# Two squared-ReLU MLPs on one TensorEngine: sums of h behind the next bank, the last set's work spread over seven down units, operands' highs ahead of the weights' highs

## The chip, the cores and the metric

The kernel runs on one core of one Trainium2 chip. The metric is the device time of one execution in microseconds (us). TensorE is PE below, VectorE DVE, ScalarE ACT, GpSimd POOL, SyncE SP.

## The reference

Two layers of a streaming encoder, each a mixer and an MLP, for 1024 prompt frames and 64 sample frames that share the weights. The change touches the MLPs alone:

```
def squared_relu_mlp(h, w_up, w_down):
    return jnp.square(jax.nn.relu(h @ w_up)) @ w_down

h = rms_norm(x, norm_g[i, 2])
x = x + rms_norm(squared_relu_mlp(h, mlp_w_up[i], mlp_w_down[i]), norm_g[i, 3])
```

With D_MODEL 1024 and D_FF 4096 an MLP turns 1088 frames of 1024 values into 4096 and back. All is fp32. The kernel makes each fp32 product out of three passes over two fp32r parts of each operand, a high (the operand rounded by a cast) and a low (the operand less its high): high by high, high by low, low by high.

## The kernel before

Frames are in columns, 1088 of them: T, in halves of 544 or in blocks of 384, 384 and 320. Class Mlp writes one MLP, and its methods tensor, scalar, vector, gpsimd and sync write what each engine does, in a fixed order. Engines wait for each other through counting semaphores; nothing is scheduled but by this code. The program has two MLPs (near 570 to 1290 us and 1700 to 2410 us).

**First wave and plain tiles.** The 32 tiles of 128 hidden values come in three kinds. FIRST_TILES, four of them, are made block by block in four banks while the norm of the next block still runs; DVE takes each bank (relu, L1620), ACT squares it (L1411). During the last block (b == NB - 1) ACT also writes three scaled copies of h for each pair k of its tiles (gain, L1389), and DVE makes from them the four sums of h that Strassen's scheme (in Winograd's form, seven products in place of eight) needs (sums_of_h, L1502 to L1509). Then come two PLAIN_TILES (dense_set, L314), on banks 0 to 2 and 5 to 7. PE begins the first of them when three of the last four first banks are taken and the lows of its weights are ready: cast by ACT (ws.high, L224), subtracted on POOL (ws.low, L230). Behind the plain tiles DVE makes the lows of the sums (L1513) and takes the plain banks (L1542), and the first double set begins (product, L1205).

**Double sets.** The other 26 tiles are 13 double sets (DOUBLES) of seven products each (N_PROD, product i in one of four slots of two banks). DVE combines them to the four blocks of the result (combine, L1552), takes relu (L1556, L1574), ACT squares (L1393), and DVE makes three sums and a difference of them (sums_of_act, L1530 to L1535). SP stores all to memory (store_set).

**Down.** The second matrix is worked in 7 groups (GROUPS) of 4 units (PAIRS), numbered d = 4g + p. A unit is again seven products of 12 matmuls, 1.5 us each at full clock, some 10.5 us a unit. Each product is added to y by DVE (take_product, L1600 for the first, L1604), which frees its slot for a later product: the take of product 0 is waited for by product 3 of the same unit, 1 by 4, 2 by 6, 3 and 4 by 0 and 1 of the next unit, 5 by its 5, 6 by its 2.

Each group needs seven operands (pieces), which SP loads one group ahead (load_piece), ACT casts to highs (high_piece, L1397), and DVE turns to lows (low_piece, L1513). Each unit needs one unit of weights, which SP loads when product 4 of the unit two before is done (load_pair, L210); POOL mixes it for Strassen's scheme (mix, L240 to L245), ACT casts it in two parts, the blocks as loaded (L251) and the mixed ones (L253), and POOL makes the lows (low_pair, L261). The last group loads the four first tiles in place of pieces (load_first, high_first, low_first), and its units end with turn_back, two subtractions on y (L1612).

What matters for the order: the last set's relus and sums are done in one go, the relus at the end of the last double set, the four sums behind the whole of down unit 0. In a down unit ACT casts the weights first and the pieces behind them. DVE subtracts the pieces at the places of this table, which counts as (p, i), behind the take of product i:

```
{(1, 2): 0, (1, 5): 1, (2, 1): 2, (2, 3): 3, (2, 5): 4, (3, 2): 5, (3, 5): 6}
```

Of the kernel before, what the change touches and what calls it, by code (L numbers as in the profile page):

```python
# [10 lines left out]
ALU = mybir.AluOpType  # L11
# [129 lines left out]
class WeightStream:  # L141
# [105 lines left out]
    def high_pair(self, act, unit):  # L247
# [3 lines left out]
        self.chip.nc.scalar.copy(hi[:, 0, QUARTER:UNIT], raw[:, 0, QUARTER:UNIT]).then_inc(self.pair_hi, 1)  # L251
        act.wait_ge(self.mixed, 3 * self.pair(unit) + 3)
        self.chip.nc.scalar.copy(hi[:, 1], raw[:, 1]).then_inc(self.pair_hi, 1)  # L253

# [770 lines left out]
class Mlp:  # L1025
# [25 lines left out]
    STEPS = 13  # L1051
# [37 lines left out]
    def step(self, n, k):  # L1089

        return self.steps(self.DOUBLE_STEP) + self.STEPS * n + k

# [207 lines left out]
    def sync(self, sp):  # L1300
# [61 lines left out]
        for g in range(GROUPS):  # L1362
            for p in range(PAIRS):
                d = PAIRS * g + p
                if g < GROUPS - 1 and p < 2:
                    for i in ((0, 1, 2), (3, 4, 5, 6))[p]:
                        load_piece(g + 1, i)
                elif p < 2:
                    for j in (2 * p, 2 * p + 1):
                        load_first(j)  # L1370
                sp.wait_ge(self.prod_full, self.down_count(d, 4))
                if d < PAIRS * GROUPS - 2:
                    ws.load_pair(sp, self.down_unit(d + 2))
                    if d == 0:
                        store_set(DOUBLES)
                    continue
# [5 lines left out]
    def scalar(self, act):  # L1382
# [49 lines left out]
        for n in range(DOUBLES):  # L1432
# [6 lines left out]
            last = n == DOUBLES - 1  # L1439
            ws.high_pair(act, self.down_unit(0) if last else self.double_unit(n + 1, 0))  # L1440
            if last:
                high_piece(0, 0)
            act.wait_ge(self.stepped, self.step(n, self.C11_TAKEN))
            square(self.act[:, 0])
            if last:
                high_piece(0, 1)
                high_piece(0, 2)
            else:
                ws.high_pair(act, self.double_unit(n + 1, 1))
            act.wait_ge(self.stepped, self.step(n, self.C12_TAKEN))  # L1450
            square(self.act[:, 2])
            if last:
                high_piece(0, 3)
            act.wait_ge(self.stepped, self.step(n, self.C22_TAKEN))
            square(self.act[:, 3])
            if last:
                high_piece(0, 4)
            act.wait_ge(self.stepped, self.step(n, self.C21_TAKEN))
            square(self.act[:, 1])
        high_piece(0, 5)  # L1460
        high_piece(0, 6)

        for g in range(GROUPS):
            for p in range(PAIRS):
                d = PAIRS * g + p
                if d < PAIRS * GROUPS - 1:
                    ws.high_pair(act, self.down_unit(d + 1))
                if g < GROUPS - 1:
                    for i in ((), (0, 1, 2), (3, 4), (5, 6))[p]:
                        high_piece(g + 1, i)  # L1470
                else:
                    for j in ((), (0, 1), (2, 3), ())[p]:
                        high_first(j)
# [19 lines left out]
    def vector(self, dve):  # L1493
# [30 lines left out]
        def sums_of_act(n, squares):  # L1524
# [3 lines left out]
            dve.wait_ge(self.squared, squares)  # L1528
            dve.wait_ge(self.a_out, self.outs(n))
            nc.vector.tensor_tensor(s1, a21, a22, ALU.add).then_inc(self.stepped, 1)  # L1530
            nc.vector.tensor_tensor(a21, a21, a11, ALU.subtract).then_inc(self.stepped, 1)
            dve.wait_ge(self.stepped, self.step(n - 1, self.SUM1))
            nc.vector.tensor_tensor(s2, s1, a11, ALU.subtract).then_inc(self.stepped, 1)
            dve.wait_ge(self.stepped, self.step(n - 1, self.SUM2))
            nc.vector.tensor_tensor(s4, s2, a12, ALU.subtract).then_inc(self.stepped, 1)  # L1535
# [23 lines left out]
        def double_until_c21(n):  # L1559

            c22, banks, last = self.halves(self.c22[:]), self.slot_banks, n == DOUBLES - 1
# [22 lines left out]
            relu(n, a12, a12, 0, self.C12_RAW)  # L1584
            relu(n, a22, self.c22[:], 1, self.C22_FULL)
            if last:
                low_piece(0, 3)
            full(n, 6)
            combine(n, self.C21_RAW, a21, c22, banks(6), ALU.subtract)
            relu(n, a21, a21, 1, self.C21_RAW)  # L1590
# [24 lines left out]
        for b in range(NB):  # L1615
            self.before.keep_ready(dve, b)
            for j in range(FIRST_TILES):
# [6 lines left out]
                if b == NB - 1:  # L1624
                    sums_of_h(j)
# [10 lines left out]
        sums_of_act(0, self.squares(PLAIN_TILES))  # L1636
        for n in range(DOUBLES):
            double_until_c21(n)
            if n < DOUBLES - 1:
                sums_of_act(n + 1, self.double_squares(n, 4))  # L1640

        for d in range(PAIRS * GROUPS):
            g, p = divmod(d, PAIRS)
            for i in range(self.N_PROD):
                take_product(d, i)
                if d == 0 and i < 3:
                    low_piece(0, 4 + i)
                if g < GROUPS - 1:
                    piece = {(1, 2): 0, (1, 5): 1, (2, 1): 2, (2, 3): 3, (2, 5): 4, (3, 2): 5, (3, 5): 6}.get((p, i))
                    if piece is not None:  # L1650
                        low_piece(g + 1, piece)
# [1699 lines left out]
```

## Time and profile before

| | us |
|---|---|
| median of 3 runs | 2456.99 |
| lowest and highest | 2453.17, 2457.27 |
| time of the profiled execution | 2461.53 |
| its span | 2459.7 |
| PE busy, share of the span | 2356.7, 96% |
| DVE busy | 1599.3, 65% |
| ACT busy | 1015.4, 41% |
| POOL busy | 966.1, 39% |
| mean granted clock of PE | 0.984 |

The span runs from the first to the last instruction of the profiled execution; 1.8 us lie around it. Busy is the time in which at least one instruction of the engine ran. The granted clock is the share of its 2.4 GHz that PE was given.

### The profile page before, as it was taken

To read this page: it belongs to the slowest core of one execution; us is meant where nothing else is said; L and a number is where in the kernel's file an instruction comes from. 1 tells how busy PE (TensorE), PEld (TensorE's weight loads), DVE (VectorE), ACT (ScalarE), POOL (GpSimd) and SP (SyncE) were. 2 spreads that over 40 slices of the span, in tenths; PEclk is the share of its full clock that TensorE was granted. 3 is DMA by queue.
4 is the path that set the end of the run, shared out by engine and by line. 5 is a ranking of instruction groups with operands and counts; after the bars stand their busy time and mean duration, and the time that the engine had idled before them with its cause. 6 is when DMAs were issued, how large, how long until landed. Compare 5 with 4: busy or idle time off the path is not lost.

```text
span 2459.7 us, 46195 instructions
## 1 busy us (share of the span) xinstructions
PE 2356.7 (96%) x18814; PEld 2215.0 (90%) x18814; DVE 1599.3 (65%) x2469; ACT 1015.4 (41%) x1910; POOL 966.1 (39%) x580
## 2 busy tenths in 40 slices
PE   8999999999899998999999999999999999999997
PEld 7888887799899998999999877689999999999997
DVE  6554454417777778778768344426687778787886
ACT  5554544536433334333326455536533334333321
POOL 0101020115344445677746200114244445677663
PEclk9999999999999999999999999899999999999999
DMA  3101011015243336343325100014323435434334
GB/s 114 44 10 59 19 42 35 30 48 162 94 147 146 146 138 225 134 151 107 133 74 162 60 21 27 26 35 130 123 107 147 146 147 192 163 123 162 115 109 133
DMA packets 117695, 257.42 MB, mean 105 GB/s; under 512 B 11264, under 2 KB 42240, under 8 KB 117536
## 3 DMA queue, kind: packets, MB, share of 16 engines
q1 hardware_dynamic: 109664, 248.62, 29.3%
q10 hardware_dynamic: 7808, 6.56, 0.9%
q8 instruction: 102, 1.67, 0.3%
q14 instruction: 57, 0.47, 0.1%
q0 software_dynamic: 64, 0.10, 0.0%
HBM read 176.79 MB, written 78.45 MB: 104 GB/s over the span
## 4 chain that ended last, share of the span: by engine, by line
PE 68%; DVE 12%; issue 7%; ACT 5%; DMA 4%; POOL 3%; ACTq 0%; SPq 0%; DVEq 0%; POOLq 0%
PE banks L1205 28%; PE banks L298 25%; PE banks L2446 4%; DMA w_raw<-in_units 4%; DVE y L1604 3%; POOL w_raw L240 1%; DVE mlp_s_lo L1513 1%; PE banks L2581 1%; ACT w_hi L253 1%; PE banks L2600 1%; PE banks L1956 1%; PE banks L1937 1%; PE banks L1924 1%; POOL w_raw L243 1%; ACT mlp_s_raw L1389 1%
## 5 line engine op out<-in xcount | busy, mean ns | idle before, releaser
L298 PE MATMUL banks<-h_hi,w_hi 128*128 128x384 f32 (+1 forms) x1416 | 487.8, 344 | 3.7 <-DVE w_lo L269 1.4
L298 PE MATMUL banks<-h_lo,w_hi 128*128 128x384 f32 (+1 forms) x1416 | 467.8, 330 | 0.0
L298 PE MATMUL banks<-h_hi,w_lo 128*128 128x384 f32 (+1 forms) x1416 | 467.2, 330 | 0.0
L230 POOL TENSOR_TENSOR w_lo<-w_raw,w_hi 128x1024 fp32r<-128x1024 f32 x56 | 139.1, 2483 | 800.7 <-ACT w_hi L224 800.7
L261 POOL TENSOR_TENSOR w_lo<-w_raw,w_hi 128x768 fp32r<-128x768 f32 (+1 forms) x164 | 372.4, 2293 | 184.5 <-DVE w_raw L245 147.2
L1604 DVE TENSOR_TENSOR y<-banks,y 128x544 f32<-128x544 f32 x360 | 259.9, 722 | 96.1 <-PE banks L1205 79.5
L1205 PE MATMUL banks<-h_hi,w_hi 128*128 128x272 f32 x1312 | 275.0, 291 | 28.1 <-DVE y L1604 10.2
L298 PEld LDWEIGHTS banks<-h_hi,w_hi 128*128 128x128 f32 x1416 | 268.1, 189 | 27.0 <-issue 18.6
L1205 PE MATMUL banks<-h_lo,w_hi 128*128 128x272 f32 x1312 | 272.2, 289 | 0.0
L1205 PE MATMUL banks<-h_hi,w_lo 128*128 128x272 f32 x1312 | 272.0, 289 | 0.0
L298 PEld LDWEIGHTS banks<-h_lo,w_hi 128*128 128x128 f32 x1416 | 268.3, 189 | 1.9
L298 PEld LDWEIGHTS banks<-h_hi,w_lo 128*128 128x128 f32 x1416 | 267.7, 189 | 0.0
L1205 PEld LDWEIGHTS banks<-h_hi,w_hi 128*128 128x128 f32 x1312 | 205.7, 189 | 33.0 <-DVE y L1600 10.1
L1205 PE MATMUL banks<-mlp_s_hi,w_hi 128*128 128x272 f32 x984 | 207.8, 293 | 16.8 <-DVE y L1604 13.5
L1205 PEld LDWEIGHTS banks<-h_lo,w_hi 128*128 128x128 f32 x1312 | 207.3, 190 | 0.0
L1205 PEld LDWEIGHTS banks<-h_hi,w_lo 128*128 128x128 f32 x1312 | 206.4, 190 | 0.0
L1205 PE MATMUL banks<-mlp_s_hi,w_lo 128*128 128x272 f32 x984 | 204.1, 290 | 0.0
L1205 PE MATMUL banks<-mlp_s_lo,w_hi 128*128 128x272 f32 x984 | 203.1, 288 | 0.0
L253 ACT CAST w_hi<-w_raw 128x1024 fp32r<-128x1024 f32 x82 | 86.3, 1053 | 266.2 <-POOL w_raw L245 157.8
L261 POOL TENSOR_TENSOR wide_lo<-wide_raw,wide_hi 128x768 fp32r<-128x768 f32 (+1 forms) x52 | 118.1, 2292 | 146.3 <-DVE wide_raw L245 146.3
L1205 PEld LDWEIGHTS banks<-mlp_s_hi,w_hi 128*128 128x128 f32 x984 | 154.4, 190 | 23.2 <-DVE y L1604 16.3
L251 ACT CAST w_hi<-w_raw 128x768 fp32r<-128x768 f32 x82 | 68.4, 834 | 245.4 <-DMA w_raw<-in_units 245.4
(252 smaller groups left out, 5054.4 us busy)
## 6 DMA issues: line engine op xcount, KB each, us to landing
w_raw<-in_units SPq DMA_DIRECT2D x154, 512.0 KB, 3.7
sets_scratch<-mlp_act SPq DMA_DIRECT2D x28, 1088.0 KB, 4.2
h_raw<-sets_scratch SPq DMA_DIRECT2D x56, 544.0 KB, 5.3
sets_scratch<-mlp_act_sums SPq DMA_DIRECT2D x28, 816.0 KB, 5.0
mlp_s_raw<-sets_scratch SPq DMA_DIRECT2D x42, 544.0 KB, 6.4
wide_raw<-in_units SPq DMA_DIRECT2D x26, 512.0 KB, 4.4
x_scratch<-y SPq DMA_DIRECT2D x48, 192.0 KB, 2.4
norm_x<-x_scratch SPq DMA_DIRECT2D x28, 192.0 KB, 3.2
```

Of the source, the lines that this page charges most:

```text
L230: c.nc.gpsimd.tensor_tensor(c.w_lo[:, s], c.w_raw[:, s], c.w_hi[:, s].bitcast(F32), ALU.subtract).then_inc(self.ready, 1)
L240: ops.tensor_tensor(two(to[:, 0:2 * QUARTER]), of(raw, 0)[:, None, :].to_broadcast([P, 2, QUARTER]), two(raw[:, QUARTER:3 * QUARTER]), ALU ...
L243: ops.tensor_tensor(of(to, 2), of(raw, 2), of(to, 0), ALU.subtract).then_inc(self.mixed, 1)
L251: self.chip.nc.scalar.copy(hi[:, 0, QUARTER:UNIT], raw[:, 0, QUARTER:UNIT]).then_inc(self.pair_hi, 1)
L253: self.chip.nc.scalar.copy(hi[:, 1], raw[:, 1]).then_inc(self.pair_hi, 1)
L261: self.chip.nc.gpsimd.tensor_tensor(lo[:, i, at], raw[:, i, at], hi[:, i, at].bitcast(F32), ALU.subtract).then_inc(self.pair_ready, 1)
L298: mm = chip.nc.tensor.matmul(out, w, x, start=(first and n == 0), stop=(last and n == 2))
L1205: mm = nc.tensor.matmul(chip.banks[:, bank + c, 0:half], w, x[:, c * half:(c + 1) * half], start=(not prod.adds and n_k == 0 and m == 0), ...
L1389: nc.scalar.activation(self.operand(i, k, None, self.s_raw), chip.y[:, 2 * k + tile, self.HALVES[half]], ACT.Copy, scale=gains[tile]).then ...
L1513: nc.vector.tensor_tensor(out, raw, high.bitcast(F32), ALU.subtract).then_inc(self.a_ready, 1)
L1604: nc.vector.tensor_tensor(y, bank, y, ALU.add).then_inc(self.y_added, 1)
L2446: mm = nc.tensor.matmul(out, x, y, start=(k == 0 and i == 0), stop=(k == KT - 1 and i == 2))
```

## The change

Nothing is computed in another way, and no instruction's shape changes. Five things move, in both MLPs:

1. First wave, last block: sums_of_h(j) stands behind the take of bank j + 1 rather than of bank j; on ACT gain(j) stands ahead of the wait for bank j's take, and the casts of the two plain units come behind banks 2 and 3 rather than 1 and 2.
2. The last set (n == DOUBLES - 1): its three late relus go from the end of the set to down units 0, 1 and 2 (behind product 6 of unit 0, else behind product 3), its four sums from behind unit 0 to units 3, 4, 5 and 6. ACT's last four squares go to units 0 to 3. step() is renumbered to fit, and SP stores the last set at unit 8 in place of unit 0.
3. ACT in down units: the pieces' highs stand ahead of the weights' highs. In the last set the blocks of down unit 1 are cast ahead of pieces 5 and 6 (high_blocks), its mixed part behind them (high_mixed).
4. DVE in down units: the lows of pieces stand behind products 1 and 5 of units p = 1, 2, 3, and the seventh behind product 1 of the next group's first unit, so no unit has more than two.
5. SP loads pieces 0 to 3 in a group's first unit and 4 to 6 in its second, rather than 0 to 2 and 3 to 6.

```diff
@@ step
+        if isinstance(n, int) and n == DOUBLES - 1:
+            k = {self.C21_RAW: self.C12_TAKEN, self.C12_TAKEN: self.C22_TAKEN, self.C22_TAKEN: self.C21_RAW}.get(k, k)
@@ sync
-                    for i in ((0, 1, 2), (3, 4, 5, 6))[p]:
+                    for i in ((0, 1, 2, 3), (4, 5, 6))[p]:
                         load_piece(g + 1, i)
...
-                    if d == 0:
+                    if d == 2 * PAIRS:
                         store_set(DOUBLES)
@@ scalar
                 n = FIRST_TILES * b + j
+                if b == NB - 1:
+                    gain(j)
                 act.wait_ge(self.first_taken, self.firsts(n + 1))
...
-                if b == NB - 1:
-                    gain(j)
-                    if j in (1, 2):
-                        ws.high(act, u0 + FIRST_TILES + j - 1)
+                if b == NB - 1 and j > 1:
+                    ws.high(act, u0 + FIRST_TILES + j - 2)
...
+        ws.high_pair(act, self.down_unit(0))
+        for i in range(5):
+            high_piece(0, i)
+        ws.high_blocks(act, self.down_unit(1))
+        for i in range(5, self.N_PROD):
+            high_piece(0, i)
...
+                if p == 0 and g:
+                    high_piece(g, 6)
+                if p and g < GROUPS - 1:
+                    for i in (2 * p - 2, 2 * p - 1):
+                        high_piece(g + 1, i)
+                elif p in (1, 2):
+                    for j in (2 * p - 2, 2 * p - 1):
+                        high_first(j)
+                if 0 < d < PAIRS * GROUPS - 1:
                     ws.high_pair(act, self.down_unit(d + 1))
...
+                elif d == 0:
+                    ws.high_mixed(act, self.down_unit(1))
+                if g == 0:
+                    i, taken = last_squares[p]
+                    act.wait_ge(self.stepped, self.step(DOUBLES - 1, taken))
+                    square(self.act[:, i])
@@ vector
-                if b == NB - 1:
-                    sums_of_h(j)
+                if b == NB - 1 and j:
+                    sums_of_h(j - 1)
+        sums_of_h(FIRST_TILES - 1)
...
+                if d < self.LAST_STEPS and i == (6 if d == 0 else 3):
+                    last_set(d)
                 if d == 0 and i < 3:
                     low_piece(0, 4 + i)
+                if g and p == 0 and i == 1:
+                    low_piece(g, 6)
                 if g < GROUPS - 1:
...
+                    if p and i in (1, 5):
+                        low_piece(g + 1, 2 * (p - 1) + (i == 5))
...
-            if d == 0:
-                sums_of_act(DOUBLES, self.double_squares(DOUBLES - 1, 4))
```

PE and POOL have the same instructions in the same order as before. DVE, last block of the first wave of the first MLP, before: each bank's take (mlp_first_act<-banks) is followed by the four sums of h.

```order
L1620 SCALAR_TENSOR_TENSOR mlp_first_act<-banks,keep 128x320
L1502 SCALAR_TENSOR_TENSOR mlp_s_raw<-y,gains,mlp_s_raw 128x544
L1504 SCALAR_TENSOR_TENSOR mlp_s_raw<-y,gains,mlp_s_raw 128x544
L1507 TENSOR_TENSOR mlp_s_raw<-mlp_s_raw 128x544
L1509 TENSOR_TENSOR mlp_s_raw<-mlp_s_raw 128x544
L1620 SCALAR_TENSOR_TENSOR mlp_first_act<-banks,keep 128x320
```

The same place of DVE now:

```order
L1654 SCALAR_TENSOR_TENSOR mlp_first_act<-banks,keep 128x320 x2
L1513 SCALAR_TENSOR_TENSOR mlp_s_raw<-y,gains,mlp_s_raw 128x544
L1515 SCALAR_TENSOR_TENSOR mlp_s_raw<-y,gains,mlp_s_raw 128x544
L1518 TENSOR_TENSOR mlp_s_raw<-mlp_s_raw 128x544
L1520 TENSOR_TENSOR mlp_s_raw<-mlp_s_raw 128x544
L1654 SCALAR_TENSOR_TENSOR mlp_first_act<-banks,keep 128x320
```

The third bank's take has one block of sums ahead of it, where it had two. DVE, end of down unit 0 and start of unit 1, before (y<-banks is a take, mlp_act_sums and mlp_act<-mlp_act the last set's sums):

```order
L1600 COPY y<-banks 128x544 x2
L1604 TENSOR_TENSOR y<-banks,y 128x544
L1600 COPY y<-banks 128x544
L1530 TENSOR_TENSOR mlp_act_sums<-mlp_act 128x544
L1531 TENSOR_TENSOR mlp_act<-mlp_act 128x544
L1533 TENSOR_TENSOR mlp_act_sums<-mlp_act_sums,mlp_act 128x544
L1535 TENSOR_TENSOR mlp_act_sums<-mlp_act_sums,mlp_act 128x544
L1600 COPY y<-banks 128x544
L1604 TENSOR_TENSOR y<-banks,y 128x544 x2
L1513 TENSOR_TENSOR h_lo<-h_raw,h_hi 128x2x544
```

And now:

```order
L1634 COPY y<-banks 128x544 x2
L1638 TENSOR_TENSOR y<-banks,y 128x544
L1634 COPY y<-banks 128x544
L1575 SCALAR_TENSOR_TENSOR mlp_act<-mlp_act,keep 128x544
L1634 COPY y<-banks 128x544
L1638 TENSOR_TENSOR y<-banks,y 128x544
L1524 TENSOR_TENSOR h_lo<-h_raw,h_hi 128x2x544
L1638 TENSOR_TENSOR y<-banks,y 128x544
L1634 COPY y<-banks 128x544
L1575 SCALAR_TENSOR_TENSOR mlp_act<-mlp_c_103,keep 128x544
L1634 COPY y<-banks 128x544
```

One relu stands where four sums stood, and the next unit has one relu more. ACT, down units 1 and 2, before (w_hi a cast of weights, h_hi and mlp_s_hi casts of pieces):

```order
L251 CAST w_hi<-w_raw 128x768
L253 CAST w_hi<-w_raw 128x1024
L1397 CAST h_hi<-h_raw 128x2x544 x2
L1397 CAST mlp_s_hi<-mlp_s_raw 128x2x544
L251 CAST w_hi<-w_raw 128x768
L253 CAST w_hi<-w_raw 128x1024
```

And now, in the units of a later group:

```order
L1407 CAST h_hi<-h_raw 128x2x544 x2
L251 CAST w_hi<-w_raw 128x768
L256 CAST w_hi<-w_raw 128x1024
L1407 CAST mlp_s_hi<-mlp_s_raw 128x2x544
L1407 CAST h_hi<-h_raw 128x2x544
L251 CAST w_hi<-w_raw 128x768
```

The pieces' casts, which stood behind the mixed weights' cast, stand ahead of both casts of the unit.

## Rows read from the trace of the kernel before

**Rows 1.** The page's part 1: busy us (share of the span) and instructions of each engine.

```profile
PE 2356.7 (96%) x18814; PEld 2215.0 (90%) x18814; DVE 1599.3 (65%) x2469; ACT 1015.4 (41%) x1910; POOL 966.1 (39%) x580
```

**Rows 2.** Waits of PE: who waited for whom, us in total, times, longest us.

```profile
PE banks L1205 <- DVE y L1604: 23.7, 32, 1.6
PE banks L1205 <- DVE y L1600: 11.7, 6, 3.0
PE banks L314 <- DVE mlp_first_act L1620: 8.6, 2, 4.3
PE banks L1205 <- DVE mlp_act L1542: 6.5, 2, 4.4
...
PE banks L1205 <- DVE h_lo L1513: 1.8, 2, 0.9
```

**Rows 3.** Windows: us; busy of PE, PEld, DVE, ACT, POOL; granted clock; DMA.

```profile
639.00:649.00 10.00, 9.98 (x46) 10.00 (x47) 5.39 (x5) 5.41 (x9) 2.74 (x1) 0.75 0.55 195
667.50:677.50 10.00, 9.95 (x67) 9.95 (x68) 7.07 (x10) 5.63 (x8) 2.75 (x2) 0.83 0.16 55
986.90:996.90 10.00, 9.91 (x60) 9.91 (x61) 6.28 (x9) 3.04 (x3) 4.18 (x2) 0.73 0.19 46
1766.70:1776.70 10.00, 9.97 (x51) 10.00 (x52) 5.43 (x5) 5.37 (x9) 2.77 (x1) 0.83 0.56 197
1796.90:1806.90 10.00, 9.97 (x67) 9.97 (x68) 7.10 (x11) 5.64 (x8) 0.93 (x1) 0.83 0.28 91
2092.10:2102.10 10.00, 10.00 (x58) 10.00 (x59) 6.58 (x8) 0.56 (x1) 1.54 (x1) 0.70 0.97 356
```

**Rows 4.** Timeline of DVE, first wave: start, us, line, operation [idle before <- releaser].

```profile
634.97 2.74 DVE L1507 TENSOR_TENSOR mlp_s_raw<-mlp_s_raw 128x544 f32<-128x544 f32 x1
...
638.39 0.48 DVE L1620 SCALAR_TENSOR_TENSOR mlp_first_act<-banks,keep 128x320 f32<-128x320 f32 x1
```

**Rows 5.** Timeline of PE, the first matmuls of the first plain tile.

```profile
639.02 1.24 PE L314 MATMUL banks<-h_hi,w_hi 128*128 128x384 f32 x3 [4.31 <-DVE mlp_first_act L1620]
```

**Rows 6.** Timeline of ACT, last block of the first wave.

```profile
625.54 2.02 ACT L1389 ACTIVATE mlp_s_raw<-y,gains 128x544 f32<-128x544 f32 x3
...
633.33 1.03 ACT L224 CAST w_hi<-w_raw 128x1024 fp32r<-128x1024 f32 x1
```

**Rows 7.** Timeline of POOL, lows of the first plain unit.

```profile
634.44 2.70 POOL L230 TENSOR_TENSOR w_lo<-w_raw,w_hi 128x1024 fp32r<-128x1024 f32 x1 [16.25 <-ACT w_hi L224]
```

**Rows 8.** Timeline of DVE behind the first wave: lows of the sums, first plain take.

```profile
655.21 11.03 DVE L1513 TENSOR_TENSOR mlp_s_lo<-mlp_s_raw,mlp_s_hi 128x1632 fp32r<-128x1632 f32 x4
666.16 1.34 DVE L1542 SCALAR_TENSOR_TENSOR mlp_act<-banks,keep 128x768 f32<-128x768 f32 x2
```

**Rows 9.** Timeline of DVE, the last set's sums in down unit 1.

```profile
955.98 1.44 DVE L1530 TENSOR_TENSOR mlp_act_sums<-mlp_act 128x544 f32<-128x544 f32 x1
...
961.95 0.71 DVE L1600 COPY y<-banks 128x544 f32<-128x544 f32 x1
```

**Rows 10.** Timeline of DVE, lows of pieces in down units 4 and 5.

```profile
996.27 1.28 DVE L1513 TENSOR_TENSOR h_lo<-h_raw,h_hi 128x1088 fp32r<-128x1088 f32 x1
...
1013.41 3.33 DVE L1513 TENSOR_TENSOR h_lo<-h_raw,h_hi 128x1088 fp32r<-128x1088 f32 x1 [0.61 <-ACT h_hi L1397]
...
1018.95 2.39 DVE L1513 TENSOR_TENSOR h_lo<-h_raw,h_hi 128x1088 fp32r<-128x1088 f32 x1
```

**Rows 11.** Timeline of POOL, the weights of down unit 6.

```profile
1008.36 1.30 POOL L240 TENSOR_TENSOR w_raw<-w_raw 128x512 f32<-128x512 f32 x1 [3.11 <-DMA w_raw<-in_units]
...
1011.37 4.23 POOL L261 TENSOR_TENSOR w_lo<-w_raw,w_hi 128x768 fp32r<-128x768 f32 x2
```

**Rows 12.** Timeline of PE, down unit 6, product 0.

```profile
1022.03 0.52 PE L1205 MATMUL banks<-mlp_s_hi,w_hi 128*128 128x272 f32 x2 [1.02 <-DVE y L1604]
```

**Rows 13.** Timeline of ACT, pieces' highs behind the weights' in down unit 5.

```profile
1012.28 2.10 ACT L1397 CAST h_hi<-h_raw 128x1088 fp32r<-128x1088 f32 x2
```

**Rows 14.** The page's part 6, pieces' loads: xcount, KB each, median us to landing.

```profile
h_raw<-sets_scratch SPq DMA_DIRECT2D x56, 544.0 KB, 5.3
```

More of the change, by code:

```diff
@@ L251, in high_pair, with high_mixed @@
         self.chip.nc.scalar.copy(hi[:, 0, QUARTER:UNIT], raw[:, 0, QUARTER:UNIT]).then_inc(self.pair_hi, 1)
+    def high_mixed(self, act, unit):
+        hi, _, raw = self.tiles(self.place(unit))
         act.wait_ge(self.mixed, 3 * self.pair(unit) + 3)
         self.chip.nc.scalar.copy(hi[:, 1], raw[:, 1]).then_inc(self.pair_hi, 1)
+    def high_pair(self, act, unit):
+        self.high_blocks(act, unit)
+        self.high_mixed(act, unit)
     def low_pair(self, pool, unit):
@@ L1438, in scalar @@
             nc.scalar.copy(self.halves(self.c22[:]), self.slot_banks(0)).then_inc(self.copied, 1)
[L1439 to L1442, printed above, removed]
+            if n == DOUBLES - 1:
+                break
+            ws.high_pair(act, self.double_unit(n + 1, 0))
             act.wait_ge(self.stepped, self.step(n, self.C11_TAKEN))
             square(self.act[:, 0])
[L1445 to L1461, printed above, removed]
+            ws.high_pair(act, self.double_unit(n + 1, 1))
+            for i, taken in ((2, self.C12_TAKEN), (3, self.C22_TAKEN), (1, self.C21_TAKEN)):
+                act.wait_ge(self.stepped, self.step(n, taken))
+                square(self.act[:, i])
[5 more added lines that the diff above has]
+            high_piece(0, i)
+        last_squares = ((0, self.C11_TAKEN), (2, self.C12_TAKEN), (3, self.C22_TAKEN), (1, self.C21_TAKEN))
         for g in range(GROUPS):
@@ L1583, in double_until_c21, with last_set @@
             combine(n, self.C12_RAW, a12, c22, banks(4), ALU.subtract, self.C22_FULL)
-            relu(n, a12, a12, 0, self.C12_RAW)
-            relu(n, a22, self.c22[:], 1, self.C22_FULL)
             if last:
                 low_piece(0, 3)
+            else:
+                relu(n, a12, a12, 0, self.C12_RAW)
+                relu(n, a22, self.c22[:], 1, self.C22_FULL)
             full(n, 6)
             combine(n, self.C21_RAW, a21, c22, banks(6), ALU.subtract)
-            relu(n, a21, a21, 1, self.C21_RAW)
+            if not last:
+                relu(n, a21, a21, 1, self.C21_RAW)
+        def last_set(n):
+            a11, a21, a12, a22 = (self.act[:, i] for i in range(4))
+            if n == 0:
+                relu(DOUBLES - 1, a12, a12, 0, self.C12_RAW)
+            elif n == 1:
+                relu(DOUBLES - 1, a22, self.c22[:], 1, self.C22_FULL)
+            elif n == 2:
+                relu(DOUBLES - 1, a21, a21, 1, self.C21_RAW)
+            else:
+                sum_of_act(DOUBLES, n - 3)
         def take_product(d, i):
@@ L1635, in vector @@
         take_plain(1)
-        sums_of_act(0, self.squares(PLAIN_TILES))
+        sums_of_act(0)
         for n in range(DOUBLES):
@@ L1639, in vector @@
             if n < DOUBLES - 1:
-                sums_of_act(n + 1, self.double_squares(n, 4))
+                sums_of_act(n + 1)
         for d in range(PAIRS * GROUPS):
```

40 lines of the change are left out of this document (19 added, 21 removed).

## The prediction

> **What bounds the kernel now.** I read the page first, then PE's waits, the windows, and the timelines of the places that the waits name. PE is busy for 2356.7 of 2459.7 us [rows 1], so any gain has to come out of the 103 us in which PE stands, or out of time at a lower clock. The waits of PE say who keeps it [rows 2]. Five kinds lie in what the change touches: takes of down products (L1604, 23.7 us in 32 waits, and L1600, 11.7 in 6), lows of pieces (L1513, 1.8), the third first-tile bank (L1620, 8.6 in 2), and the first plain bank (L1542, 6.5 in 2). That is 52.3 us, all of it waits for DVE, though DVE is busy for only 65% of the span: it is late, not overfull. Behind the long stops PE's granted clock is below 1. Six windows of 10 us have 0.75, 0.83, 0.73, 0.83, 0.83 and 0.70 [rows 3], that is a part of each at 1.2 GHz and the rest at 2.4. PE is busy throughout them, so each costs 10 x (1 - clock): 2.5, 1.7, 2.7, 1.7, 1.7 and 3.0, together 13.3 us. So 65.6 us are there to be had.
>
> **First wave and plain tiles.** PE stands 4.31 us ahead of the first plain tile, until the take at 638.39 [rows 4, 5]. That take stood behind two blocks of sums, and each block waited for ACT's copies (2.02 us, [rows 6]), one of its operations also for POOL, whose first plain lows run from 634.44 to 637.14 (2.74 us for that operation, [rows 4, 7]). Now one block stands ahead of the third take, and its copies come before the takes. The third bank was full one product before 634.7 (24 matmuls of 320 columns, 3.2 us at 2.4 GHz), at about 631.3, so it is taken by 632. But then something else is last: the lows of the plain weights. ACT casts them behind the square of bank 2, at about 632.2 to 633.2 (before: 633.33, [rows 6]), and POOL needs 2.7 us [rows 7]. PE starts at about 636.1 and still stands 1.4 of the 4.3 us.
>
> The next stop is no longer set there. The double sets begin when DVE has taken the first plain bank, behind four lows (11.03 us, [rows 8]). The whole chain on DVE moves forward. Its lows began at 655.2 [rows 8], some 3 us of mixing behind the last sum. Now the four blocks of sums run at about 3.0 us each (four operations of 0.7 to 0.8) from 628.2, with two short takes and one or two waits for POOL of 2 us between them. That gives about 645, and the lows at 648: 7 us earlier, in both MLPs alike, and the double sets start 7.0 us earlier, at 660.5 in the first. PE itself gets there at 636.1 + 24.0 = 660.1: before, it ran from 639.0 until 2.1 us before the take's end at 667.5, which is 26.4 us [rows 2, 5, 8], less 2.5 of clock. Term: 2 x 7.0 = **14.0 us**, clock of the plain tiles included. Ends: 5 each if DVE's lows meet POOL worse (they took 1.5 us more in the second MLP), 7.4 if PE's own arrival decides. Behind it PE lost 1.7 us of clock twice [rows 3]. The stop shrinks from 2.0 to about 0.4 in the first MLP, and from 4.4 to some 2 in the second. I count one of the two: **1.7 us**.
>
> **Last set's relus and sums.** Before, four sums stand ahead of unit 1's first take and last from 955.98 to 961.95, 6.0 us with the waits for POOL [rows 9]. PE stands for the first take 3.0 us [rows 2]. The three late relus delay the lows of pieces 3 to 6 too (the 1.8 us of L1513). All seven are now single operations of 0.7 us, at most one to a unit. The take of product 3 is asked for by the next unit's first product 4.5 us later, so 0.7 us, or 0.7 + 2.4 behind the longer of POOL's two lows (4.23 together, [rows 11]), fits. What is moved on SP: store_set goes from unit 0 to unit 8. Its 1.9 MB stood ahead of the weights of unit 3, which came late. At unit 8 it stands ahead of unit 9's three pieces and the weights of unit 11, which may land some 2 us later; these have 3.6 us to spare (below). ACT's squares are waited for only by the sums, three units on. Cost nothing.
>
> **Steady down units.** In unit 5 the first low waits 0.61 us for ACT, because the piece's cast stands behind the weights' mixed cast [rows 10, 13], and then for POOL: 3.33 us for what took 1.28 at 996.27, since POOL works from 1011.37 to 1015.60 [rows 10, 11]. The next low at 1018.95 also takes 2.39, and product 2 of unit 6 stands 1.02 us [rows 12] for the take of product 6. Units with three lows do the same. Now the piece is cast a unit ahead, and no unit has three lows. By these rows, counted from a unit's start: take 1 ends at 3.75, where POOL is between its mix and its lows. If DVE wins, its low ends at 5.0, if POOL wins at 6.9; take 2 ends at 7.6 at the latest and is asked for at 9.0. The low behind take 5 falls from 9.7 to 11.0, when POOL is idle (it starts the next mix at 11.3). Take 6 ends at 11.7 and is asked for at 13.5. Hence no stop in a plain unit. In units 1 to 6 a relu or sum makes three again. The same reckoning leaves 0.3 us for take 6 when all three meet POOL. Before, such units stood some 1 us [rows 12]; I let 5 of 12 do so: 5 us remain. The last group's lows come earlier on ACT by the same move. Term: 23.7 + 11.7 + 1.8 - 5.0 = **32.2 us**, ends 18 (half stays) and 37. With the cluster of long stops in units 1 to 3 gone, its clock returns: 2.7 + 3.0 = **5.7 us**, ends 0 and 5.7.
>
> What the order costs the weights: on ACT two casts of pieces (2.10 us, [rows 13]) stand ahead of the weights' casts. They run before the weights land, since POOL waits 3.1 us for its load in each unit [rows 11]. If not: POOL's lows end at 1015.6 and product 1 of unit 6 needs them at 1019.2, so 3.6 us are free.
>
> **Sum**: 14.0 + 1.7 + 32.2 + 5.7 = 53.6 us. The profiled execution took 2461.5, 4.5 above the median of 2457.0; against the median, **2403.4 us**.
>
> **Rivals.** *The stops move to POOL's port.* Rows show that a DVE operation with two inputs in SBUF waits for POOL's running instruction [rows 10, 11], while one that reads banks does not. If meetings are worse than reckoned, each of the 14 moved operations costs 1 us, and the 36 units with two lows 0.3 each: 25 stay in place of 5, and 2423; with the clock's 5.7 gone too, 2429. The Trainium skill, "SBUF — State Buffer", section "Who interferes with whom", says that a DVE instruction with two SBUF inputs and a GpSimd one that reads SBUF exclude each other for a whole instruction. The trace agrees (3.33 us against 1.28). By that rule alone, 14 operations that each wait 2.4 us put up to 33 us back on DVE, and the result would be near 2437 if none of it were covered. For the forecast speaks that every take has 1.8 to 4.5 us before it is asked for.
>
> *The clock stays low.* The shorter stops might still be followed by 1.2 GHz. In the trace stops near 1 us in down units left it at 1, but a 2.0 us stop gave a window of 0.83 [rows 2, 3]. Without any clock 2411; inside the forecast.
>
> *Nothing gained*: another chain as late as DVE's, POOL's lows, stands just behind, and stops keep their length under another name. Against: 3.6 us free. 2457.
>
> *Slower*: ACT stops in order at a piece that has not landed, and the weights' casts, POOL's lows and PE queue behind it. A piece takes 5.3 us to land [rows 14] and is issued over 10 us before its turn. To decide, 36 units would have to lose over 1.5 us each beyond the 3.6 free, pieces some 5 us behind ACT's turn. At 6 us: 36 x 2.4 = 86 us more, 2490.
>
> **Chances.** Forecast (2390 to 2412) 0.64; port 0.23 (2412 to 2437); nothing gained 0.06, of which 0.04 within 0.2%; slower 0.05; lower than 2390 0.02. About 0.2% (5 us) is what a measurement of this kernel tells from no change. Faster 0.91, same 0.04, slower 0.05. Range 2390 to 2430: it takes in the forecast and most of the port's case.
>
> **What would show it.** PE's waits for L1620 (now L1654) near 3 us or put down to the plain weights' lows; waits for L1542 under 3; those for takes under 10 in all, with none above 1.5; windows behind the old stops at 0.95 and up; takes of product 6 less than 1.8 us behind their banks in steady units. Wrong: waits named after POOL's or ACT's w_lo and w_hi, DVE lows still at 3.3 us with stops behind them, or a long stop at units 10 and 11.

## The result, and the profile after

| | us |
|---|---|
| changed kernel, median of 4 runs | 2389.09 |
| lowest and highest | 2385.79, 2392.34 |
| kernel before, median of 4 runs | 2457.13 |
| ratio, 95% interval | 0.9721, 0.9695 to 0.9747 |
| its profiled execution, its span | 2392.34, 2390.6 |

The change takes off 68.0 us, where 53.6 were forecast. The sign and the mechanisms were right. The time is 0.9 us below the low end of the range, so the gain was mis-sized. The term that failed is the one of the down units' stops: each stop was priced at its idle row alone, and costs some 0.27 us more (below).

The page's part 1 and the first line of its part 4 (the chain of waits by engine), as in [rows 1]:

```profile
PE 2334.2 (98%) x18814; PEld 2203.1 (92%) x18814; DVE 1540.5 (64%) x2469; ACT 1015.4 (42%) x1910; POOL 980.7 (41%) x580
...
PE 87%; DVE 8%; issue 2%; ACT 2%; ACTq 0%; DMA 0%; POOL 0%; SPq 0%; DVEq 0%; POOLq 0%
```

PE's idle time fell from 103 us to 56. DVE does the same 2469 instructions and is busy 58.8 us less: it spends less time inside operations that wait for POOL. PE's waits, with the columns of [rows 2]:

```profile
PE banks L506 <- DVE norm_diag L737: 6.0, 6, 1.8
...
PE banks L321 <- POOL w_lo L230: 2.9, 2, 1.4
...
PE banks L1215 <- DVE y L1638: 2.2, 4, 0.9
...
PE banks L1215 <- DVE h_lo L1524: 0.4, 2, 0.2
```

The takes' 35.4 us of [rows 2] (23.7 and 11.7) are 2.2 us. The third first-tile bank is no longer waited for (8.6 us before), nor is the first plain bank (6.5). What stands in place of the former is the plain weights' lows, 1.4 us each, as predicted to the tenth. The largest wait left belongs to a norm, which the change does not touch.

Windows behind the places of [rows 3], same columns. The last is 60 us of down units:

```profile
637.70:647.70 10.00, 9.91 (x59) 9.91 (x60) 9.81 (x12) 3.56 (x4) 2.91 (x2) 1.00 0.55 164
665.30:675.30 10.00, 9.88 (x78) 9.85 (x79) 8.61 (x14) 2.35 (x3) 0.00 (x0) 1.00 0.36 136
940.00:1000.00 60.00, 60.00 (x483) 59.94 (x482) 50.86 (x57) 24.82 (x28) 50.05 (x28) 1.00 0.51 180
```

All are at the full 2.4 GHz, and the second MLP's are too. In those 60 us of down units PE does not stop once.

The first wave on DVE's timeline (start, us), against [rows 4, 8]:

```profile
632.87 0.49 DVE L1654 SCALAR_TENSOR_TENSOR mlp_first_act<-banks,keep 128x320 f32<-128x320 f32 x1
...
635.55 2.77 DVE L1520 TENSOR_TENSOR mlp_s_raw<-mlp_s_raw 128x544 f32<-128x544 f32 x1
...
649.57 11.04 DVE L1524 TENSOR_TENSOR mlp_s_lo<-mlp_s_raw,mlp_s_hi 128x1632 fp32r<-128x1632 f32 x4
660.54 1.34 DVE L1561 SCALAR_TENSOR_TENSOR mlp_act<-banks,keep 128x768 f32<-128x768 f32 x2
```

The third bank is taken at 632.87, not at 638.39. One sum still waits 2 us inside its operation for POOL. The four lows take the same 11.0 us as in [rows 8], but begin 5.6 us earlier, and the first plain bank is free (661.88) just before PE comes for it (661.94), without a stop.

And DVE's groups by shape, in 200 us of down units (xcount, busy us, mean ns, idle before):

```profile
L1524 DVE TENSOR_TENSOR h_lo<-h_raw,h_hi 128x1088 fp32r<-128x1088 f32 x19 | 30.8, 1621 | 0.0
L1524 DVE TENSOR_TENSOR mlp_s_lo<-mlp_s_raw,mlp_s_hi 128x1088 fp32r<-128x1088 f32 x15 | 22.1, 1474 | 0.0
```

Of the kernel before, the same in 1000 to 1210 us:

```profile
L1513 DVE TENSOR_TENSOR h_lo<-h_raw,h_hi 128x1088 fp32r<-128x1088 f32 x19 | 43.5, 2289 | 3.3 <-ACT h_hi L1397 3.3
L1513 DVE TENSOR_TENSOR mlp_s_lo<-mlp_s_raw,mlp_s_hi 128x1088 fp32r<-128x1088 f32 x14 | 33.2, 2375 | 4.0 <-ACT mlp_s_hi L1397 4.0
```

A low costs 1.5 to 1.6 us instead of 2.3 to 2.4, and none waits for ACT. This pair of views says most about the down units.

**Where the 69.1 us of span went.** I cut PE's timeline at three events: the end of the first wave's last matmul, the first matmul of the double sets, and the end of the last down matmul. S1 is the stretch between the first two, S2 between the last two. Every experiment below is read the same way. A stop is a row of PE's timeline with more than 0.1 us of idle before it, and that idle is what its row says.

| | S1, first and second MLP | S2 | stops in S2, their idle us |
|---|---|---|---|
| before | 32.84, 34.51 | 597.77, 596.41 | 23 and 23, 20.2 and 18.3 |
| after | 25.58, 25.58 | 569.20, 569.20 | 3 and 3, 1.3 and 1.3 |
| gain | 7.3 + 8.9 = 16.2 | 28.6 + 27.2 = 55.8 | |

The rest of the program took 2.9 us more, in stretches whose order is unchanged. In a later profile of the same kernel (below) the first wave ended 2.8 us earlier than in this one, so such a difference is within what they vary.

### The profile page after: what moved, and what is told of

Same layout as the page of the kernel before. It is cut to its first block, busy times and chain, and to the rows that moved or that the text cites. A ratio compares the mean times of both kernels' runs of the same rounds, so it can differ in the third digit from the quotient of the medians.

```text
span 2390.6 us, 46195 instructions
## 1 busy us (share of the span) xinstructions
PE 2334.2 (98%) x18814; PEld 2203.1 (92%) x18814; DVE 1540.5 (64%) x2469; ACT 1015.4 (42%) x1910; POOL 980.7 (41%) x580
## 4 chain that ended last, share of the span: by engine, by line
PE 87%; DVE 8%; issue 2%; ACT 2%; ACTq 0%; DMA 0%; POOL 0%; SPq 0%; DVEq 0%; POOLq 0%
PE banks L1215 45%; PE banks L305 26%; PE banks L2482 4%; DVE mlp_s_lo L1524 1%; PE banks L2617 1%; PE banks L2636 1%; PE banks L1992 1%; PE banks L1973 1%; DVE y L1638 1%; PE banks L1960 1%; PE banks L2000 1%; PE banks L2626 1%; DVE norm_acc L697 1%; DVE y L748 1%; PE banks L2601 1%
## 5 line engine op out<-in xcount | busy, mean ns | idle before, releaser
L268 POOL TENSOR_TENSOR w_lo<-w_raw,w_hi 128x768 fp32r<-128x768 f32 (+1 forms) x164 | 410.6, 2524 | 169.5 <-DVE w_raw L245 144.0
```

What stands on the lines that cost most here:

```text
L268: self.chip.nc.gpsimd.tensor_tensor(lo[:, i, at], raw[:, i, at], hi[:, i, at].bitcast(F32), ALU.subtract).then_inc(self.pair_ready, 1)
```

## The experiments

Two theories stood at the start. A: each part gives what its removed idle and its clock say, plus something that every stop costs and no wait row shows. B: the excess over the forecast came from one place, such as the clock or the wave. The mechanism, that DVE is late because it waits for ACT's order and for POOL's port, had to be shown as well.

### e1_wave: part 1 alone

```diff
 before.py, scalar
+                if b == NB - 1:
+                    gain(j)
                 act.wait_ge(self.first_taken, self.firsts(n + 1))
...
 vector
-                if b == NB - 1:
-                    sums_of_h(j)
+                if b == NB - 1 and j:
+                    sums_of_h(j - 1)
+        sums_of_h(FIRST_TILES - 1)
```

> The kernel before with the first part of the change alone (sums of h behind the next bank, gains ahead of the takes, plain weights cast behind banks 2 and 3). Theory A, that PE's stops cost what their idle rows say plus about 0.28 us each (the overlap of back-to-back matmuls and the restart) plus the clock behind them: the stretch from the first wave's end to the first double set goes from 32.8 and 34.5 us to 25.6 in both MLPs, and the stretch behind it, without its clock of 0.83, loses some 1.7 us each: in all 20 us less, near 2437. Theory B, that the parts only work together because DVE is late for another reason as well: less than half of it, 2447 or more.

Measured: 2438.96 against 2460.14, ratio 0.9926 (0.9903 to 0.9948), 21.2 us off. S1 is 25.59 in both MLPs, S2 593.10 and 594.87 with 23 and 21 stops. The wave is worth its 16 us by itself. The rest lies in S2, most of it clock: the window at the double sets' start is at 1.00 here, and three windows behind stops in S2 (0.84, 0.83, 0.83) give 5.0 us where the four of [rows 3] in S2 gave 9.1. Theory A had 20 us.

### e2_steady: parts 3 to 5 alone

```diff
 before.py, scalar
-                if d < PAIRS * GROUPS - 1:
-                    ws.high_pair(act, self.down_unit(d + 1))
-                if g < GROUPS - 1:
-                    for i in ((), (0, 1, 2), (3, 4), (5, 6))[p]:
+                if p == 0 and g:
+                    high_piece(g, 6)
+                if p and g < GROUPS - 1:
+                    for i in (2 * p - 2, 2 * p - 1):
                         high_piece(g + 1, i)
...
+                if d < PAIRS * GROUPS - 1:
+                    ws.high_pair(act, self.down_unit(d + 1))
 sync
-                    for i in ((0, 1, 2), (3, 4, 5, 6))[p]:
+                    for i in ((0, 1, 2, 3), (4, 5, 6))[p]:
 vector
+                if g and p == 0 and i == 1:
+                    low_piece(g, 6)
...
-                    piece = {(1, 2): 0, (1, 5): 1, (2, 1): 2, (2, 3): 3, (2, 5): 4, (3, 2): 5, (3, 5): 6}.get((p, i))
+                    if p and i in (1, 5):
+                        low_piece(g + 1, 2 * (p - 1) + (i == 5))
```

> The kernel before with parts 3 to 5 alone (pieces' highs ahead of the weights', two lows to a unit, pieces 0 to 3 and 4 to 6), the last set as before. Theory A: some 16 stops in each MLP from down unit 5 on go, 12 us of idle rows and 16 x 0.28 of uncounted time each, in all 31 to 33 us less, near 2425. Theory C, that idle rows are the whole price of a stop: 24 us less, near 2433. The 3.0 us stop behind the last set's sums stays, and with it perhaps the clock of 0.73 and 0.70 behind it.

Measured: 2417.59 against 2460.14, ratio 0.9834 (0.9809 to 0.9858), 42.6 us off, some 10 more than theory A had and 19 more than theory C. Of 23 stops an MLP, four and five are left. The long one is the wait behind the four sums, still there because part 2 is not:

```profile
958.20 0.41 PE L1205 MATMUL banks<-mlp_s_lo,w_hi 128*128 128x272 f32 x2
958.45 0.41 PE L1205 MATMUL banks<-mlp_s_hi,w_lo 128*128 128x272 f32 x2
961.88 0.52 PE L1205 MATMUL banks<-h_hi,w_hi 128*128 128x272 f32 x2 [3.02 <-DVE y L1602]
```

The window behind it:

```profile
961.90:971.90 10.00, 10.00 (x80) 10.00 (x81) 8.57 (x11) 0.75 (x1) 2.16 (x2) 1.00 0.85 305
```

In e1_wave a stop of the same length has:

```profile
954.70:964.70 10.00, 9.97 (x68) 9.97 (x69) 7.38 (x9) 0.59 (x1) 1.57 (x1) 0.84 0.99 358
```

So the stops at unit 3, which I had put down to the last set, went with the steady order alone, but for one of 0.22 us. The clock behind the 3.0 us stop happened to stay up.

### e3_lastset: part 2 alone

```diff
 after.py, vector (the wave, ACT's order in down units and SP's loads are put back in the same way)
-                if g and p == 0 and i == 1:
-                    low_piece(g, 6)
...
-                    if p and i in (1, 5):
-                        low_piece(g + 1, 2 * (p - 1) + (i == 5))
+                    piece = {(1, 2): 0, (1, 5): 1, (2, 1): 2, (2, 3): 3, (2, 5): 4, (3, 2): 5, (3, 5): 6}.get((p, i))
+                    if piece is not None:
+                        low_piece(g + 1, piece)
```

> The kernel before with part 2 alone (relus and sums of the last set spread over units 0 to 6, its ACT order, the store at unit 8), first wave and steady order of before. Theory A: the stops of units 0 to 4 (8.1 us of rows in the first MLP), their uncounted 0.28 each and the clock behind them (2.7 and 3.0 us) go, 22 us in all, near 2435. Rival: units that already have three lows get a fourth operation, and 12 units stand 1 us longer each: 10 us less only, near 2447.

Measured: 2449.22 against 2460.14, ratio 0.9958 (0.9943 to 0.9973), 10.9 us off. This is the rival's case. The 3.0 us stop is gone, but product 2 now waits 0.94, 1.02 and 1.10 us in units 2, 3 and 4, behind units in which DVE has two or three lows and one operation of the last set more. Alone, the spread pays part of its gain back. Beside the table with two lows to a unit and ACT's new order it does not: in the changed kernel no take makes PE wait in units 1 to 25. The three parts alone give 21.2 + 42.6 + 10.9 = 74.7; together they give 68.0 to 71.6, so they overlap little.

### e4_weights_first: the changed kernel with the weights' highs first

```diff
 after.py, scalar
+                if 0 < d < PAIRS * GROUPS - 1:
+                    ws.high_pair(act, self.down_unit(d + 1))
+                elif d == 0:
+                    ws.high_mixed(act, self.down_unit(1))
                 if p == 0 and g:
                     high_piece(g, 6)
...
-                if 0 < d < PAIRS * GROUPS - 1:
-                    ws.high_pair(act, self.down_unit(d + 1))
-                elif d == 0:
-                    ws.high_mixed(act, self.down_unit(1))
```

> The changed kernel with ACT casting the weights ahead of the pieces again, all else as changed. Theory A: the pieces' highs of a unit come behind the mixed weights' cast, some 4.8 us into the unit, so the low behind take 1 is late, misses POOL's pause between mix and lows, and take 2 comes about 1 us too late for product 6: 36 stops of 1 us and 0.28, near 2435. Rival, that the order on ACT is worth nothing as long as no unit has three lows: 2389.

Measured: 2461.36 in one run, so the whole gain is gone. Each MLP has 45 stops in S2 (23.4 and 25.5 us idle); S2 is 602.88 and 606.40. In 1000 to 1210 us, by shape:

```profile
L1524 DVE TENSOR_TENSOR h_lo<-h_raw,h_hi 128x1088 fp32r<-128x1088 f32 x19 | 48.9, 2572 | 12.1 <-ACT h_hi L1407 12.1
L1524 DVE TENSOR_TENSOR mlp_s_lo<-mlp_s_raw,mlp_s_hi 128x1088 fp32r<-128x1088 f32 x14 | 41.0, 2927 | 13.4 <-ACT mlp_s_hi L1407 13.4
```

ACT, POOL and DVE in one unit (this kernel's timeline, engine by engine):

```profile
1007.61 1.06 ACT L256 CAST w_hi<-w_raw 128x1024 fp32r<-128x1024 f32 x1 [3.19 <-POOL w_raw L245]
1008.57 1.09 ACT L1407 CAST mlp_s_hi<-mlp_s_raw 128x1088 fp32r<-128x1088 f32 x1
...
1007.65 4.22 POOL L268 TENSOR_TENSOR w_lo<-w_raw,w_hi 128x768 fp32r<-128x768 f32 x2
...
1009.70 3.33 DVE L1524 TENSOR_TENSOR mlp_s_lo<-mlp_s_raw,mlp_s_hi 128x1088 fp32r<-128x1088 f32 x1 [1.24 <-ACT mlp_s_hi L1407]
```

The mixed cast waits for POOL's mix. What stands behind it comes just when POOL starts its lows, and DVE's low then waits 1.2 us for ACT and 2 us inside its operation for POOL. I had expected 46 of these 72 us. With all else as changed, the order on ACT decides whether anything is gained.

### e5_old_table: the changed kernel with the old places of the lows

```diff
 after.py, scalar
-                    for i in (2 * p - 2, 2 * p - 1):
+                    for i in ((), (0, 1), (2, 3, 4), (5, 6))[p]:
-                if p == 0 and g:
-                    high_piece(g, 6)
...
 vector: the table of before, in place of the lows behind takes 1 and 5
```

> The changed kernel with the lows of pieces on DVE at their old places (three in units p = 2) and ACT casting them just ahead, before the weights. Theory A: units with three lows stand again, about 0.3 to 1 us in 12 to 24 of them, near 2400. Rival, that the places are worth nothing once ACT is on time: 2389.

Measured: 2404.72 in one run; 7 and 8 stops, S2 574.93 and 577.29. The lows take 1.9 us on average here, and none waits for ACT. So ACT's order carries most of the steady part and the places the rest, some 16 us by the totals and 13.8 by S2.

### e8_pool_writes: is it POOL's port?

The kernel before, with POOL's lows of the double and down weights replaced by a memset. This leaves out the low parts of those weights. POOL then has less to do too, and reads less.

```diff
 before.py, low_pair
-            self.chip.nc.gpsimd.tensor_tensor(lo[:, i, at], raw[:, i, at], hi[:, i, at].bitcast(F32),
-                                              ALU.subtract).then_inc(self.pair_ready, 1)
+            self.chip.nc.gpsimd.memset(lo[:, i, at].bitcast(F32), 0.0).then_inc(self.pair_ready, 1)
```

> The kernel before with POOL's lows of the double and down weights replaced by memsets to zero (low parts of these weights are left out of the products). POOL then reads SBUF only in its mixing. Port theory: the lows on DVE that took 3.3 and 2.4 us take 1.3 to 2, the stops from unit 5 on fall from some 16 an MLP to under 5, 25 us or more less, 2430 or below. Rival, that DVE is late because of ACT's order: lows still start late, stops stay, 2450 or more.

Measured: 2409.26 against 2459.09, one run each. S1 is 30.43 and 29.92, S2 576.19 and 574.74, with 6 and 4 stops. In 1000 to 1200 us:

```profile
L1512 DVE TENSOR_TENSOR h_lo<-h_raw,h_hi 128x1088 fp32r<-128x1088 f32 x20 | 25.7, 1284 | 3.4 <-ACT h_hi L1396 3.4
L1512 DVE TENSOR_TENSOR mlp_s_lo<-mlp_s_raw,mlp_s_hi 128x1088 fp32r<-128x1088 f32 x15 | 19.3, 1288 | 3.4 <-ACT mlp_s_hi L1396 3.4
```

Every low takes its bare 1.28 us, though DVE's and ACT's order is that of before. That is 50 us with nothing moved. One low there runs beside a memset, 1011.94 to 1013.22:

```profile
1011.94 1.28 DVE L1512 TENSOR_TENSOR mlp_s_lo<-mlp_s_raw,mlp_s_hi 128x1088 fp32r<-128x1088 f32 x1
```

```profile
1012.00 0.74 POOL L261 MEMSET w_lo<- 128x768 f32 x1
```

It is not held up. The 15 lows that overlap a memset in this trace take 1.28 to 1.33 us; the 53 that overlap only the subtractions of L261 in the trace of before take 1.28 to 3.35, 2.62 on average. The Trainium skill, "SBUF — State Buffer", section "Who interferes with whom", says that a DVE instruction with two SBUF inputs contends with a GpSimd one that reads SBUF and not with one that only writes; the trace agrees, at 1.28 us beside a memset and 3.33 beside a subtraction. Since POOL is also busy for less time here (624.1 us, not 966.1), it is these overlaps that separate port from load, not the total.

### e6_stops6 and e7_stops5: what a stop costs

The changed kernel, with six or five more additions on DVE that read product 0's bank, ahead of its take, in the first unit of groups 3, 4 and 5. Their results are used nowhere. They make three stops an MLP of a known length.

```diff
 after.py, take_product
+            if i == 0 and p == 0 and 3 <= d // PAIRS <= 5:
+                dve.wait_ge(self.a_out, self.outs(SETS))
+                for out in [self.act[:, n] for n in range(4)] + [self.act_sums[:, n] for n in range(6 - 4)]:
+                    nc.vector.tensor_tensor(self.halves(out), bank, self.halves(chip.keep[:, first]), ALU.add)
```

> The changed kernel with six more operations on DVE (each adds a bank and keep into space that is free by then, 0.65 us apart) ahead of the take of product 0 in the first unit of groups 3, 4 and 5 of both MLPs: work that the result does not need. PE then stands at product 3, some 1.6 us by its idle row. Theory A: the stretch from the first product of the double sets to the last of the down units grows from 569.2 by three times the idle row plus 0.28, to about 574.8. Theory C: by three times the idle row, to about 574.0.

> As the run with six, with five more operations: the stops are 0.65 us shorter, about 1.0 us by their rows. Theory A: the stretch is three times the row plus 0.28 above 569.2, about 573.0; the difference between row and cost is the same as with six. Theory C: about 572.2. If the uncounted part grew with the stop, it would be half as large here as with six.

Measured: 2401.76 and 2391.42, one run each, with stops of 1.69 and 1.06 us. From one made stop to the next, four units on, it is 43.85 and 43.21 us in the traces: 0.64 us more for 0.63 us more idle. So a longer stop costs just its longer row. Every stop costs something beside it, too. In both profiles of the changed kernel, without made stops, the same four units take 41.87 us: the stops cost 1.98 and 1.34 us, 0.29 and 0.28 more than their rows.

By the lengths that were expected the two theories could not be told apart: S2 is 574.72 and 573.64 with six operations (A 574.8, C 574.0), 571.82 and 571.73 with five (A 573.0, C 572.2). The 569.2 from which both counted holds a stop of 0.93 us at unit 27 that only the first of these four has. The totals say less still: 4.8 of the 10.3 us between them lie in S2, the rest where the edit does nothing. PE's timeline of e7_stops5:

```profile
1061.93 0.41 PE L1215 MATMUL banks<-mlp_s_lo,w_hi 128*128 128x272 f32 x2
1062.18 0.41 PE L1215 MATMUL banks<-mlp_s_hi,w_lo 128*128 128x272 f32 x2
1063.65 0.52 PE L1215 MATMUL banks<-h_hi,w_hi 128*128 128x272 f32 x2 [1.06 <-DVE y L1642]
1064.00 0.41 PE L1215 MATMUL banks<-h_lo,w_hi 128*128 128x272 f32 x2
```

A pair of matmuls lasts 0.41 us, but the next pair starts 0.25 behind it. The row's 1.06 us count from the end of the last pair (1062.18 + 0.41 = 1062.59), which lies 0.16 behind the time at which the next would have started. Behind the stop the first pair takes 0.35 us to the next one, 0.10 more than 0.25. Together 0.26. The ends of matmuls are modelled in these views, so how the 0.26 us divide is less sure than their sum, which rests on starts. From 1062.18 to 1064.00 it is 1.82 us where 0.50 would do: 1.32, not 1.06.

The lengths of S2 agree. The second MLP of the changed kernel's second run (below) is 567.94 with 0.35 us idle. Against it e7_stops5 has 571.73 with 3.39, so 0.75 us over three stops are not in the rows, 0.25 each; e6_stops6 has 573.64 with 5.29, 0.25 each. The 43 additional stops of each MLP of e4_weights_first give 0.28 and 0.27, once the 1.6 us of clock behind a stop of 3.51 us in its second MLP (window 0.84) are taken off. Over all 24 MLPs of the twelve traces, S2 less its idle and its clock is 567.1 us and 0.27 more for each stop, to within 0.6 us.

### after_again: the changed kernel once more

> The changed kernel once more, to stand beside the next run on the same chip: 2389, ratio 0.972.

Measured: 2386.92 (5 runs) against 2458.54 (9 runs), ratio 0.9714 (0.9701 to 0.9728). S1 is 25.59 and 25.60, S2 569.61 and 567.94. One stop of 1.6 us, for the weights of down unit 2, is new, and the 0.93 us at the end of the down units is gone. Such single stops come and go between runs; the lengths of the stretches do not change by more than 2 us.

### e9_better: can what is left be had?

```diff
 after.py, scalar
                 if b == NB - 1:
                     gain(j)
+                    if j > 1:
+                        ws.high(act, u0 + FIRST_TILES + j - 2)
...
 vector
             low(self.s_lo[:, r], self.s_raw[:, r], self.s_hi[:, r], self.operands(k + 1))
-        take_plain(0)
+            if k == 1:
+                take_plain(0)
...
+                if g == GROUPS - 1 and p and i == 3:
+                    turn_back(p - 1)
...
-            if g == GROUPS - 1:
+            if g == GROUPS - 1 and p == PAIRS - 1:
                 turn_back(p)
```

> The changed kernel with three more moves: the plain weights' casts ahead of ACT's wait for the take of banks 2 and 3, the first plain bank taken behind the second of the four lows, and turn_back of a unit behind take 3 of the next. Theory A: PE's wait for the plain lows falls from 1.43 to about 0.4, the double sets start that much earlier, and the stop of 0.93 (with its uncounted 0.28) goes: 2 x (1.0 + 1.4) = 4.8 us below the changed kernel, near 2384. Rival: DVE's chain of lows decides the start of the double sets anyway, and only turn_back's stop is gained: 2.6 us.

Measured: 2395.74 (5 runs), ratio 0.9739 (0.9724 to 0.9754), 9 us slower than the change. The plain tiles do start at once, and S1 falls to 24.13. But PE's waits now have a new first line of the MLP:

```profile
PE banks L1215 <- POOL wide_lo L268: 4.7, 2, 2.5
```

POOL has two pairs of lows to make ahead of the double sets:

```profile
654.38 7.20 POOL L268 TENSOR_TENSOR w_lo<-w_raw,w_hi 128x768 fp32r<-128x768 f32 x2 [14.91 <-ACT w_hi L251]
661.54 5.13 POOL L268 TENSOR_TENSOR wide_lo<-wide_raw,wide_hi 128x768 fp32r<-128x768 f32 x2
```

They come later themselves: 18.5 us behind the end of the first wave (654.38 against 635.89), where the changed kernel has 16.0 (652.38 against 636.36). Two of DVE's operations ahead of the last bank's take now wait for POOL (2.94 and 2.82 us), where one did:

```profile
633.51 2.94 DVE L1515 SCALAR_TENSOR_TENSOR mlp_s_raw<-y,gains,mlp_s_raw 128x544 f32<-128x544 f32 x1
...
637.24 2.82 DVE L1520 TENSOR_TENSOR mlp_s_raw<-mlp_s_raw 128x544 f32<-128x544 f32 x1
```

The take, ACT's square, the store behind it and the casts that wait for that store all follow. The double sets start 1.45 us earlier and meet lows that are 2.5 us late. Turning the result back inside the units gave stops of 0.8, 1.0 and 0.7 us, where the changed kernel has one of 0.9 in one profile and none in the other. Of the 10.8 us by which the spans differ, S1 and S2 hold 5.5; the rest lies where nothing was edited. This order does not give the 1.43 us of the plain tiles; whether another would was not tried. None of the kernels run beats the change.

## Why the prediction fell short, term by term

The profiled execution gained 69.1 us by its span. By the sum's own terms:

| term | predicted | measured |
|---|---|---|
| wave, S1 | 14.0 | 16.2 |
| idle of stops in S2 | 32.2 | 38.5 - 2.6 = 35.9 |
| clock in S2 | 1.7 + 5.7 | 9.1 |
| what a stop costs beside its row | 0 | 10.8 |
| other stretches | 0 | -2.9 |
| sum | 53.6 | 69.1 |

- **The step that failed is the down term, 23.7 + 11.7 + 1.8 - 5.0 = 32.2.** It took the idle in the rows of the waits for the whole price of a stop. For each MLP, what is left of S2's change once idle and clock are taken off is 5.3 and 5.5 us, over 20 stops that went: 0.27 us each. This is what the made stops show, 0.26 us in PE's timeline around one and 0.28 by four whole units. The same lines lay in the trace before: the duration of a pair there is 0.41 us as well, and the restart of [rows 12], which is product 2's, has 0.52.
- **The 5.0 us kept in units with three operations were not there.** The idle left is 2.2 us for takes, all of it in units 26 and 27, where turn_back stands, and none in units 1 to 6. The lows of the pieces average 1.5 to 1.6 us. Before, PE's idle in S2 also held 1.3 us of other kinds, which the sum had left out.
- **The wave's term was 2.2 us short.** The first MLP gave 7.3 for 7.0, the second 8.9. The forecast took both alike; the longer stop of 4.4 us, which the second MLP had at the start of its double sets, went entirely. PE's own arrival decided, the case for which 7.4 was given. The reckoned times held: the lows at 648 were at 649.6, and PE left the plain tiles at 661.9 for 660.1, in a profile whose first wave ended 1.6 us later than before.
- **Of the two second stops' clock I counted one and got both**, 1.7 us more. There was no stop left for the clock to follow.
- **Right:** the waits for L1620 became 1.4 us of plain lows each (predicted 1.4); no wait for L1542's take; takes under 10 us, none above 1.5; windows at 1.00; the return of the cluster's 5.7 us of clock. Moving store_set to unit 8 and the loads cost nothing that a row shows: at units 8 to 11 PE has no stop in either profile of the changed kernel.
- **The rivals:** port, nothing gained and slower did not happen. The port case is real as a mechanism (e8_pool_writes); whether the lows run into it is decided by when the highs are ready (e4_weights_first). The slower case needed ACT to be held by pieces that had not landed; [rows 14] gave 5.3 us, and 6.2 now, still far inside a unit.
- **The range** put 0.02 below 2390, because every term's upper end was reckoned in idle alone. With 0.27 us for each of the 40 stops that went, the same sum gives 10.8 us more, 2393.

What stays open: why a single wait of 1.6 us for the weights of unit 2 shows in one profile of the changed kernel and not in the other (e9_better has one of 1.4 us at the same place). Whether the 2.9 us in the other stretches are chance or the change's was not tried either.

## What to carry to other kernels

Price a stop of PE as its idle row plus the loss around it, which one timeline shows: compare the starts of the matmuls around the stop with the pitch of a running stream. Here it is 0.26 us, negligible for one stop and 11 us for 40. When an in-order engine has both casts that wait for another engine and casts that could run at once, put the free ones first: the late ones push their successor on DVE into the stretch in which POOL holds it up. Count two-input DVE operations at their price beside POOL, and choose their places by POOL's gaps.

## What the runs showed that I had not expected

**A stop's hidden part.** 0.25 to 0.29 us each, in four ways of measuring, independent of the stop's length between 1.06 and 1.69 us. The Trainium skill, "TensorE: Matmul & The Clock Gate", section "Step-by-step: what each phase is for", says that the drain of one matmul overlaps the fill of the next in a stream. That a stop loses this overlap is my reading: it fits the 0.16 us at the end of the stream, but no run here tests it, and what the other 0.10 us at the restart are, none shows.

**The clock behind a stop is not settled by the stop's length.** Eighteen stops of 1.9 to 3.9 us in seven kernels, each with the granted clock of the 10 us behind it:

| kernel | stop, clock behind it |
|---|---|
| before | 2.02: 0.83; 2.98: 1.00; 3.03: 0.70 |
| e1_wave | 3.05: 0.84; 3.05: 0.83; 1.92: 0.83 |
| e2_steady | 2.29: 0.83; 2.79: 0.84; 3.02: 1.00; 3.00: 1.00 |
| e3_lastset | 2.19: 0.83; 2.79: 1.00; 3.85: 0.74 |
| e4_weights_first | 3.51: 0.84 |
| e8_pool_writes | 2.44: 0.83; 1.92: 0.83 |
| e9_better | 2.19: 1.00; 2.52: 0.85 |

Thirteen of eighteen cost 1.5 to 3.0 us of clock, five nothing, and 2.79 us did both. Behind all six made stops of 1.69 us the windows have 1.00. A forecast can give such a stop's clock only a chance: in this kernel about 7 in 10, times 1.7 us.

**A wait inside an instruction is not in the list of waits.** DVE was busy for 1599.3 us before and 1540.5 after, with the same instructions. The 106 lows of pieces account for it: 225.2 us before, 166.0 after. With the order of before but POOL's memsets (e8_pool_writes) they take 137.5 us. So this was time at POOL's port, booked as busy. Only the mean duration by shape (2289 ns for what takes 1284) told of it.
